# The rotation of A's queries on GpSimd instead of VectorE, and their turn placed among B's maps

## The reference, cut to what matters

```python
h = rmsnorm(x, ln1_g[layer])
proj = h @ w_in[layer]
qa, ka, va, cq, ckv, kr, qc, kc, vc = jnp.split(proj, split_idx, axis=-1)
out_a = mixer_dilated(qa, ka, va, cos64, sin64)              # A: 6 heads of 64
out_b = mixer_mla(cq, ckv, kr, ..., cos32, sin32)            # B: 6 heads of 64 + 32
out_c = mixer_diff(qc, kc, vc, ..., cos32, sin32)            # C: 4 heads, two maps of 32 each
x = x + jnp.concatenate([out_a, out_b, out_c], axis=-1) @ w_o[layer]

def apply_rope(x, cos, sin):                                  # what this case calls the rotation
    half = x.shape[-1] // 2
    x1, x2 = x[..., :half], x[..., half:]
    return jnp.concatenate([x1 * cos - x2 * sin, x1 * sin + x2 * cos], axis=-1)
```

## Time and profile before

| | |
|---|---|
| three runs | 1722.94 (median), 1723.9, 1722.93 us |
| the profiled execution | 1722.32 us, its span 1720.5 us |
| granted clock of TensorE | 0.999 of full speed over the span |
| PE busy | 1708.3 us, 99% of the span |
| DVE busy | 1154.7 us, 67% |
| ACT busy | 912.6 us, 53% |
| POOL busy | 28.4 us, 2%, 32 instructions |

### The profile page before, as it was taken

How to read it: one execution, slowest core, us unless ns; L and a number is a source line. 1 busy time by engine, 2 the same in 40 slices (tenths; PEclk the granted TensorE clock), 3 DMA queues, 4 the chain that set the end, 5 groups by cost and what they waited for, 6 DMA issues and landing times.

```text
span 1720.5 us, 27260 instructions
## 1 busy us (share of the span) xinstructions
PE 1708.3 (99%) x10258; PEld 1486.1 (86%) x10258; DVE 1154.7 (67%) x1692; ACT 912.6 (53%) x1328; POOL 28.4 (2%) x32
## 2 busy tenths in 40 slices
PE   9999999999999999999999999999999999999998
PEld 8888887898888988888889888889898888989886
DVE  6665698766655766569876664678674746867473
ACT  6554456555544555445654553577553546755352
POOL 0000010000000000001000000000000000000000
PEclk9999999999999999999999999999999999999999
DMA  8854544544455554554445545544365543435551
GB/s 314 229 196 172 206 151 148 193 180 180 175 185 189 201 188 170 186 194 158 147 178 185 184 183 195 177 149 154 118 209 199 180 168 122 164 111 215 198 176 45
DMA packets 47382, 304.27 MB, mean 177 GB/s; under 512 B 5616, under 2 KB 7792, under 8 KB 13848
## 3 DMA queue, kind: packets, MB, share of 16 engines
q1 hardware_dynamic: 47256, 302.52, 49.6%
HBM read 300.02 MB, written 1.31 MB: 175 GB/s over the span
## 4 chain that ended last, share of the span: by engine, by line
PE 97%; DVE 1%; ACT 1%; issue 1%; POOLq 0%; POOL 0%; ACTq 0%; DVEq 0%
PE psG L506 14%; PE psG L508 14%; PE psG L507 14%; PE psG L586 9%; PE psP L586 6%; PE psSO L586 5%; PE psG L594 5%; PE psG L557 3%; PE psG L559 3%; PE psG L558 3%; PE psSO L594 3%; PE psP L594 3%; PE psP L627 1%; PE psSO L507 1%; PE psSO L508 1%; PE psP L508 1%
## 5 line engine op out<-in xcount | busy, mean ns | idle before, releaser
L1650 DVE TENSOR_TENSOR wlo<-raw,whi 128x1024 fp32r<-128x1024 f32 (+4 forms) x388 | 656.2, 1703 | 300.9 <-ACT whi L1130 300.7
L1130 ACT ACTIVATE whi<-raw 128x1024 fp32r<-128x1024 f32 (+4 forms) x388 | 553.2, 1443 | 275.2 <-PE psG L508 162.8
L506 PE MATMUL psG<-whi,x 128*128 128x512 f32 (+3 forms) x544 | 208.5, 383 | 0.0
L508 PE MATMUL psG<-whi,x 128*128 128x512 f32 (+3 forms) x544 | 201.0, 369 | 0.0
L507 PE MATMUL psG<-wlo,x 128*128 128x512 f32 (+3 forms) x544 | 200.5, 369 | 0.0
L506 PE MATMUL psG<-whi,hid_hi 128*128 128x512 f32 x472 | 184.0, 390 | 0.0
L508 PE MATMUL psG<-whi,hid_lo 128*128 128x512 f32 x472 | 183.6, 389 | 0.0
L507 PE MATMUL psG<-wlo,hid_hi 128*128 128x512 f32 x472 | 183.6, 389 | 0.0
L586 PE MATMUL psG<-x,whi 128*128 128x512 f32 x704 | 167.3, 390 | 0.0
L586 PEld LDWEIGHTS psG<-x,whi 128*128 128x128 f32 x704 | 130.8, 188 | 26.2
L557 PE MATMUL psG<-x,wlo 128*128 128x256 f32 x512 | 146.0, 285 | 1.4 <-DVE wlo L1650 1.4
(11 more groups left out here) (378 smaller groups left out, 2649.5 us busy)
## 6 DMA issues: line engine op xcount, KB each, us to landing
raw<-in_w SPq DMA_DIRECT2D x261, 1024.0 KB, 4.8
raw<-in_w SPq DMA_DIRECT2D x12, 768.0 KB, 4.2
raw<-in_w SPq DMA_DIRECT2D x14, 512.0 KB, 3.3
raw<-in_w SPq DMA_DIRECT2D x4, 576.0 KB, 3.5
raw<-in_w SPq DMA_DIRECT2D x4, 432.0 KB, 3.1
bias<-line_scratch SPq DMA_DIRECT2D x8, 192.0 KB, 10.2
h<-in_x SPq DMA_DIRECT2D x2, 512.0 KB, 5.4
out<-h SPq DMA_DIRECT2D x2, 512.0 KB, 2.7
```

Source lines behind the costliest of these rows:

```text
L506: e.matmul(o, ph, wh, start=first, stop=False)
L508: i = e.matmul(o, pl, wh, start=False, stop=last)
L1130: e.activation(w_at(whi, j, off, n), raw[:, j % RAW, off:off + n], ACT.Copy).then_inc(s_hi, count)
L1650: e.tensor_tensor(w_at(wlo, j, off, n), raw[:, j % RAW, off:off + n], f32(w_at(whi, j, off, n)), ALU.subtract).then_inc(s_lo, count)
```

## The change

The six instructions per half of `rope(l, "q", ...)` leave VectorE and are written out in `mixer2` of GpSimd, behind its power for `cq` and ahead of the one behind C's maps. The scratch is columns 0 to 383 of the tile `mix`, which A's results fill only after the last maps. Two semaphores are new: `s_turnq` between the multiplications and the rest, `s_rotq` when a half is rotated. The ticks and weight splits of VectorE between which the rotations stood remain. In `PREP_STEP` `"qa"` goes from step 12 to step 17, between the turn of map 8 and the scores of map 10, both of them B's; `PREP_AT` numbers ScalarE's copies accordingly. In the kernel after, the lines from the second hunk on are 2 higher up to VectorE's `mixer2`.

```diff
-ROT = {(n, t): 2 * i + t for i, n in enumerate(("kc", "qc", "kr", "q", "qb", "k")) for t in range(2)}
+ROT = {(n, t): 2 * i + t for i, n in enumerate(("kc", "qc", "kr", "qb", "k")) for t in range(2)}
...
-PREP_STEP = {0: "kc", 1: "qc", 12: "qa", 13: "kb", 14: "qb", 19: "ka"}
+PREP_STEP = {0: "kc", 1: "qc", 13: "kb", 14: "qb", 17: "qa", 19: "ka"}
...
-        PREP_AT = {"kc": 0, "qc": 1, "qa": 2, "kb": 4, "qb": 7, "ka": 10}
+        PREP_AT = {"kc": 0, "qc": 1, "kb": 2, "qb": 5, "qa": 8, "ka": 10}
...
-                if name != "kb":
-                    e.wait_ge(s_rot, rot(l, {"qa": "q", "ka": "k"}.get(name, name), 1))
+                if name == "qa":
+                    e.wait_ge(s_rotq, 2 * l + 2)
+                elif name != "kb":
+                    e.wait_ge(s_rot, rot(l, "k" if name == "ka" else name, 1))
...
                 behind(q_[1])
                 uq = [piece("mla_w_uq_2", l, (0, 1, 2), cols(g, 288)) for g in range(2)]
-                rope(l, "q", qa[:, 0, :], 6, 64, 0, 32, 0, out2(l, "q", 0))
-                tick()
-                low(NUM[uq[0]] + AHEAD, True)
-                rope(l, "q", qa[:, 1, :], 6, 64, 0, 32, 1, out2(l, "q", 1))
-                tick()
-                low(NUM[uq[0]] + AHEAD)
+                behind(uq[0])
                 behind(uq[1])
...
             def mixer2(l, nxt):
                 e.wait_ge(s_cm2, 2 * l + 2)
                 rsqrt(sm[:, 148:152], sm[:, 144:148], 4, s_cr2)
+                e.wait_ge(s_c2, 16)
+                for t in range(2):
+                    v = qa[:, t, :].rearrange("p (g w) -> p g w", w=64)
+                    cs, sn = (k2(nm, t * 32, 32).rearrange("p (o w) -> p o w", o=1).to_broadcast([128, 6, 32]) for nm in ("cos64", "sin64"))
+                    a, b = (mix[:, i, 0:384].rearrange("p (i g w) -> p i g w", i=2, g=6) for i in range(2))
+                    x1, x2 = v[:, :, 0:32], v[:, :, 32:64]
+                    e.wait_ge(s_out2, out2(l, "q", t))
+                    if t == 1:
+                        e.wait_ge(s_rotq, 2 * l + 1)
+                    e.tensor_tensor(a[:, 0], x1, cs, ALU.mult)
+                    e.tensor_tensor(a[:, 1], x2, cs, ALU.mult)
+                    e.tensor_tensor(b[:, 0], x2, sn, ALU.mult)
+                    e.tensor_tensor(b[:, 1], x1, sn, ALU.mult).then_inc(s_turnq, 1)
+                    e.wait_ge(s_turnq, 2 * l + t + 1)
+                    e.tensor_tensor(x1, a[:, 0], b[:, 0], ALU.subtract)
+                    e.tensor_tensor(x2, a[:, 1], b[:, 1], ALU.add).then_inc(s_rotq, 1)
                 e.wait_ge(s_sub, l + 1)
                 rsqrt(sm[:, 160:168], sm[:, 152:160], 8, s_subr)
```

More of the change, by code:

```diff
@@ L356, in build @@
         s_pphi, s_pplo, s_pth, s_pm = (sem(n) for n in ("s_pphi", "s_pplo", "s_pth", "s_pm"))
-        s_lams, s_lame, s_out2, s_rot, s_prep, s_cq, s_cm2, s_cr2, s_chi, s_clo = (
-            sem(n) for n in ("s_lams", "s_lame", "s_out2", "s_rot", "s_prep", "s_cq", "s_cm2", "s_cr2", "s_chi", "s_clo"))
+        s_lams, s_lame, s_out2, s_rot, s_rotq, s_turnq, s_prep, s_cq, s_cm2, s_cr2, s_chi, s_clo = (
+            sem(n) for n in ("s_lams", "s_lame", "s_out2", "s_rot", "s_rotq", "s_turnq", "s_prep", "s_cq", "s_cm2", "s_cr2", "s_chi", "s_clo"))
         s_kbr, s_mix, s_rto, s_sub, s_subr, s_c = (sem(n) for n in ("s_kbr", "s_mix", "s_rto", "s_sub", "s_subr", "s_c"))
```

## The result

| | before | after |
|---|---|---|
| median of the runs, same chips | 1722.81 us (1722.24 to 1723.92, 20 runs) | 1725.61 us (1725.06 to 1726.98, 20 runs) |
| profiled execution (span) | 1722.32 (1720.5) | 1725.95 (1724.1) |
| TensorE, VectorE, ScalarE busy | 1708.3, 1154.7, 912.6 us | 1709.6, 1151.2, 913.0 us |
| GpSimd busy | 28.4 us, 32 instructions | 43.4 us, 56 instructions |

The ratio is 1.0017, 95% interval 1.0011 to 1.0023: 2.8 us slower, which is within the 0.2% that count here as no change and inside the range, and 1.7 us above the predicted 1723.9. The interval leaves out 1.0000, so the loss is real, if small. It has the predicted sign and its forecast mechanism is there; its size is not.

The account below looks back on a forecast made before the run. TensorE's own work was taken to bound the kernel. Per layer -0.61 us for waits removed and +1.13 for a new bank wait made +0.52, +1.0 for both layers: 1723.9 us forecast, range 1721.2 to 1727.0.

Parts of the forecast that it names:

- TensorE bounds, only waits count: Whole kernel: 97% of what ended last is TensorE's own work, so shortening VectorE gains only what TensorE waits for.
- What goes, -0.61 a layer: Second mixers: without VectorE's rotation, map 7's scores are read 1.73 us earlier, removing TensorE's waits of 0.34 and 0.27 us.
- the first half: VectorE's rotation from 1159.38 to 1161.31: VectorE had waited 1.19 us before it, so dropping it was given no gain.
- What moves, cost nothing: Turn of A's queries, step 12 to 17: same 0.75 us in both places, using 0.75 of 1.30 us slack; cost nothing.
- What is added, +1.13 a layer: Step 17: scores of map 10 wait for a bank until VectorE copies map 8's turn, 1.13 us a layer.
- nothing is given back: Behind the new bank wait: the largest later wait, 0.49 us, comes 20 us on, so no recovery was counted.
- GpSimd's length: GpSimd's twelve rotation instructions a layer: TensorE waits only above 2.2 us each; a scaled estimate was 0.42 us each.
- (b): Ahead of map 7, GpSimd holds up three VectorE instructions, from 0.58 us each; full price +4.9 us, 1727.8; 5%, half 14%.
- Its half: GpSimd's hold-up just cancels the 1.73 us ahead of map 7, the 0.61 not won: +2.3 us, 1725.2; 14%.
- (a): At step 17 the new bank wait does not come and the gain stands alone: -1.2 us, 1721.7; 15%.
- (c): GpSimd's rotation is not done by step 17, over 2.2 us an instruction; at 3 us each, 1742; 1%.
- the prediction's own signs of being wrong: No wait at L907, L918 still waiting for map 7's exponential, or VectorE's splits beside GpSimd over 0.95 us or late.

Follow-up runs that it names:

- products that nobody needs: Kernel before, rotation still on VectorE, plus twelve GpSimd products of the same size into a scratch nobody reads: 1730.81 us against 1722.53 (1.0045).

## Why the prediction was right and wrong

- **TensorE bounds, only waits count.** Right. VectorE lost 24 instructions and the kernel became slower; the change of the two mixer times, and 0.6 at the end where GpSimd rotates, give every kernel's median against before to 0.5 us (0.6 for the products that nobody needs).
- **What goes, -0.61 a layer.** Here it failed. The step was "Without the rotation map 7's scores are read 1.73 us earlier ... Both go". They are read 0.34 us earlier: 1.38 of the 1.73 went back to hold-ups of VectorE's neighbours. The turn of map 7 comes 0.35 us earlier, and the wait for the `cq` copy (0.27) stays, since ScalarE's exponential, splits and `cq` copy moved by just as much as TensorE did. The size was wrong as well, the other way: both waits together cost 1.07 us by intervals and not the listed 0.61, so 0.35 of 1.07 was won. With GpSimd started later both do go, and -0.80 and -0.89 a layer is reached with the turn at step 16. Giving the first half nothing of its own was right.
- **What moves, cost nothing.** The copies of the keys were in time, as said: the fourth is done 0.81 us ahead of the turn of B's keys (1.30 before). But between the `cq` wait and that turn 0.07 + 0.16 = 0.23 us a layer were lost. A's key projection comes 0.75 us earlier to a bank that ScalarE is still emptying: it waits for the second of ScalarE's copies, begun at 1172.23 and 0.41 long, so done 0.14 us ahead of the projection's start at 1172.78, and 0.14 is also what lay between VectorE's copy and TensorE's start in the earlier trace rows. No row lists this as a wait, so the place is read and the cause is argued. In the kernel with the turn alone at step 17, +1.42 less the 1.13 of the bank and the 0.08 of the restart leaves 0.21, which answers to it.
- **What is added, +1.13 a layer.** Right in place, size (1.07 in the list, 1.13 by intervals) and cause; shown by the turn alone (1.1) and by step 16 (none). That nothing is given back was right too.
- **GpSimd's length.** That it cost TensorE nothing directly was right: 0.58 to 0.65 us each (one 1.19), far from the 2.2 at which TensorE would wait, and over by 1168.03. No row of before shows the length of a product. It came out at 0.58 and above, the very point from which rival (b) was said to decide.
- **Rivals.** (b) came true at its threshold, beside the forecast and not in place of it. Its price was set too high: each of the three instructions was held for about 0.41 us, not for a whole instruction of 0.6, but a fourth, the little product that (b) did not count, was held for 0.15. Its half gave 1725.2 and was held for 14%; that the measured 1725.6 is so near is in part luck, for (b) has neither wait gone and nothing for the moved turn and the end, and these partly cancel. The Trainium skill (SBUF — State Buffer, section Who interferes with whom) states that a VectorE instruction with two inputs in SBUF contends with a GpSimd instruction that reads SBUF and not with one that only writes it. The traces agree on both: 1.32 beside products, 0.48 beside memsets. With that rule taken as the likelier case the sum would have been +2.3. (a) is shown false by the wait, (c) by the end of the rotation. Of the prediction's own signs of being wrong one came true: VectorE's splits beside GpSimd took 1.34 us and not 0.95.
- **The sum.** Predicted 2 x (-0.61 + 1.13) = +1.0. Measured a layer: -0.35 (one wait) + 0.23 (the moved turn) + 1.13 + 0.08 = +1.09; twice that and 0.6 at the end is 2.8. The failed term makes 0.5 of the missing 1.8, the moved turn 0.5, the slow restart behind the bank wait 0.2, the end of the program 0.6. The range held the result, but of the terms only the bank wait came out as sized.

## What to carry to other kernels

Work moved from VectorE to GpSimd is worth only what VectorE's neighbours leave of it: list VectorE's instructions with two operands in SBUF in the same stretch, add up to one GpSimd instruction's length to each (0.4 us of 0.6 here), and start the GpSimd work where the next such instruction is waited for by nobody. When transposes are moved, count the banks between them and the next user first: one step of a table cost 1.3 us a layer here, and a wait that grows to 2 us can cost over 1 us more in clock. Price a wait by the interval between two marks around it, in a kernel with and one without it: the list of waits had 0.61 us where 1.07 were to be won.

## What the runs showed of the hardware

- A GpSimd product or sum of 192 numbers a partition in fp32 took 0.58 to 0.65 us in the changed kernel, one every 0.55 us; a memset of 768 numbers 0.80 us each with a semaphore between; 18 memsets of one number 0.66 us together.
- Beside GpSimd's products a VectorE instruction with both operands in SBUF took up to 0.76 us in place of 0.35 (192 numbers), up to 0.68 in place of 0.24 (96), 1.34 in place of 0.95 (768): at most some 0.4 us more, whatever the length. An instruction with one operand in PSUM kept its 0.76 for two.
- GpSimd is held as well: 1.19 us in place of 0.60 beside a split, 0.70 to 0.72 where its products alternate with VectorE's rotation.
- A VectorE product with one operand, 4 numbers a partition, took 0.23 us alone, 0.38 to 0.59 beside GpSimd's products and 0.81 beside its memsets, which hold no two-operand instruction. By the Trainium skill (SBUF — State Buffer, section Who interferes with whom) such an instruction (`tensor_scalar`) can enter a mode in which it needs the port pair that GpSimd uses, for writing too; the 0.81 agrees.
- After 2.07 us in which TensorE stood still, the granted clock from 1190.00 to 1194.50 was 0.62; after 2.04 and 2.05 us (products that nobody needs) it was 0.50 and 0.52 over some 3 us; after 1.07 and 1.94 us it stayed at 1.00.
- Idle time in the list of waits runs from the modelled end of the matmul before. Two waits listed with 0.34 and 0.27 us cost 0.50 and 0.57 by intervals.
- The first transposes began anywhere from 5.36 to 6.32 us in the traces of these kernels, whose programs are alike up to there. So two profiled spans differ by up to 1 us for what happens in the first 7 us (before and after: 0.7 of the 3.6 us between their spans), which the medians don't bear out; the mixers are therefore compared from a mark inside them.
